# Delta-rule inverse: the transposed copy Y grown by a product per level, and the orders around it redone

## The reference, cut to what matters

```python
qkv, z, a, b = jnp.split(h @ w_in, [3 * W, 4 * W, 4 * W + H], axis=-1)
qkv = jax.nn.silu(causal_depthwise_conv(qkv, conv_w))
# per chunk of tokens, with decay = exp(gcum_i - gcum_j), kb = k * beta:
a_mat = jnp.where(strict, jnp.einsum('bhncd,bhnsd->bhncs', kb, kc) * decay, 0.0)
sol = lax.linalg.triangular_solve(a_mat, rhs, left_side=True, lower=True, unit_diagonal=True)
# ... scan over the chunks gives o; then
o = rms_norm_2(o, o_norm) * jax.nn.silu(z)
h = h + rms_norm_2(o @ w_out, post_norm)
```

## Time and profile before

| | us |
|---|---|
| median of 3 runs (lowest, highest) | 893.73 (893.17, 894.28) |
| the profiled execution's own time | 893.27 |
| its span, first to last instruction | 891.1 |
| PE busy, share of the span | 881.4, 99% |
| DVE busy | 632.1, 71% |
| ACT busy | 521.7, 59% |

### The profile page before, as it was taken

One profiled execution on the slowest core, in us unless ns is written; L12 is line 12 of the kernel. 1 busy time (PEld: TensorE's weight loads), 2 busy tenths in 40 slices (PEclk: granted clock), 3 DMA queues, 4 the chain that ended last, 5 costly groups with the idle time before them and its releaser, 6 DMA issues.

```text
span 891.1 us, 13047 instructions
## 1 busy us (share of the span) xinstructions
PE 881.4 (99%) x5231; PEld 767.6 (86%) x5231; DVE 632.1 (71%) x1067; ACT 521.7 (59%) x851; POOL 38.6 (4%) x48
## 2 busy tenths in 40 slices
PE   9999999999999999999999999999999999999997
PEld 8878888888888888888888888999989987798885
DVE  7986877766575667567656556679899867767774
ACT  6997443454445677645444435466556756747782
POOL 0151000000000000000000000000014310000000
PEclk9999999999999999999999999999999999999999
DMA  8722455454745454347455654555241312654511
GB/s 313 242 95 100 185 167 211 163 193 166 248 149 188 143 189 158 126 150 242 176 194 183 223 197 150 157 177 182 65 180 49 121 46 66 219 213 142 189 48 47
DMA packets 60876, 143.72 MB, mean 161 GB/s; under 512 B 4497, under 2 KB 6673, under 8 KB 60817
## 3 DMA queue, kind: packets, MB, share of 16 engines
q1 hardware_dynamic: 60816, 142.91, 46.3%
HBM read 141.85 MB, written 1.05 MB: 160 GB/s over the span
## 4 chain that ended last, share of the span: by engine, by line
PE 95%; DVE 2%; ACT 2%; DMA 1%; issue 0%; SPq 0%; DVEq 0%
PE ps L513 90%; PE ps L521 5%; ACT arena L1467 1%; DMA raw<-mla_w_in_dram 1%; ACT whi L1467 0%; DVE arena_r L2456 0%; DVE sub L2456 0%; DVE arena L2766 0%; DVE wlo L2456 0%; ACT xhl L1467 0%; DVE X L2462 0%; DVE st L2462 0%; ACT L1470 0%; DVE arena L2456 0%; DVE xhl L2462 0%
## 5 line engine op out<-in xcount | busy, mean ns | idle before, releaser
L2456 DVE TENSOR_TENSOR wlo<-raw,whi 128x2048 fp32r<-128x2048 f32 (+4 forms) x141 | 300.0, 2137 | 104.8 <-ACT whi L1467 104.7
L1467 ACT ACTIVATE whi<-raw 128x2048 fp32r<-128x2048 f32 (+6 forms) x143 | 251.6, 1771 | 158.5 <-PE ps L513 144.0
L513 PE MATMUL ps<-xhl,whi 128*128 128x512 f32 (+1 forms) x912 | 199.6, 346 | 0.0
L513 PEld LDWEIGHTS ps<-xhl,whi 128*128 128x128 f32 x912 | 155.1, 188 | 19.9 <-DVE xhl L2462 0.2
L513 PE MATMUL ps<-whi,xhl 128*128 128x512 f32 (+2 forms) x528 | 167.2, 385 | 0.4 <-DVE xhl L2462 0.3
L513 PE MATMUL ps<-whi,oth 128*128 128x512 f32 x416 | 165.4, 398 | 0.0
L513 PE MATMUL ps<-whi,otl 128*128 128x512 f32 x416 | 162.3, 390 | 0.0
L513 PE MATMUL ps<-wlo,oth 128*128 128x512 f32 x416 | 162.1, 390 | 0.0
L513 PE MATMUL ps<-xhl,wlo 128*128 128x256 f32 x704 | 121.6, 283 | 0.0
L513 PEld LDWEIGHTS ps<-whi,xhl 128*128 128x128 f32 x528 | 98.3, 189 | 18.4 <-issue 1.8
L513 PEld LDWEIGHTS ps<-xhl,wlo 128*128 128x128 f32 x704 | 103.0, 191 | 3.2 <-DVE wlo L2456 0.2
(11 more groups left out here) (150 smaller groups left out, 827.3 us busy)
## 6 DMA issues: line engine op xcount, KB each, us to landing
raw<-mlp_w_in_dram SPq DMA_DIRECT2D x32, 1024.0 KB, 5.3
raw<-mlp_w_out_dram SPq DMA_DIRECT2D x32, 1024.0 KB, 4.9
raw<-gdn_w_in_dram SPq DMA_DIRECT2D x16, 1024.0 KB, 5.3
raw<-moba_w_qkv_dram SPq DMA_DIRECT2D x12, 1024.0 KB, 5.1
raw<-kv_w_dram SPq DMA_DIRECT2D x8, 1024.0 KB, 5.4
raw<-fox_w_in_dram SPq DMA_DIRECT2D x8, 1024.0 KB, 5.1
raw<-mla_w_o_dram SPq DMA_DIRECT2D x4, 1024.0 KB, 4.8
raw<-moba_w_o_dram SPq DMA_DIRECT2D x4, 1024.0 KB, 6.2
```

The source lines that it names most:

```text
L513: return eng.matmul(o, l, r, start=start, stop=True, skip_group_check=True)
L1467: return eng.activation(o, i, f, **kw)
L2456: return eng.tensor_tensor(o, a, b, f)
```

## The change

`inv_v` becomes a product. As X grows by X*W, its transposed Y grows by the product of W and Y; PE forms that beside `inv_x`, from the same W, and DVE adds it to Y. ACT's `inv_y(g, l)` goes. Semaphore counts follow: DVE's `s_id[g]` now counts two steps a level, ACT's `s_ia[g]` one.

```diff
             def inv_x(g, l):
                 Xb, Yb, Wb, Bb = inv_ops(g)
-                L.wait_ge(s_ia[g], 2 * l - 4)
-                b = ring(("ix", g, l), s_id[g], l + 1)
+                L.wait_ge(s_ia[g], l - 1)
+                if l > 3:
+                    L.wait_ge(s_id[g], 2 * l - 3)
+                b = ring(("ix", g, l), s_id[g], 2 * l - 2)
...
             def inv_v(g, l):
-                Xf = inv_ops(g)[0].bitcast(F32)
-                L.wait_ge(s_id[g], l + 1)
-                b = ring(("iy", g, l), s_ia[g], 2 * l - 3)
+                Xb, Yb, Wb, Bb = inv_ops(g)
+                L.wait_ge(s_ia[g], l - 1)
+                b = ring(("iy", g, l), s_id[g], 2 * l - 1)
                 for s in blk4:
-                    ins = tr(P[b][:, s], Xf[:, s])
+                    ins = mm(P[b][:, s], Wb[:, s], Yb[:, s], True)
                 ins.then_inc(s_ip[g], 1)
...
-            def inv_y(g, l):
-                L.wait_ge(s_ip[g], 3 * l - 3 - g % 2)
-                act(inv_ops(g)[1], P[bank["iy", g, l]][:, :], ACT.Copy).then_inc(s_ia[g], 1)
...
+            def inv_v(g, l):
+                Yb = inv_ops(g)[1]
+                L.wait_ge(s_ip[g], 3 * l - 3 - g % 2)
+                tt(Yb, P[bank["iy", g, l]][:, :], Yb.bitcast(F32), ALU.add).then_inc(s_id[g], 1)
```

```diff
+            hi(108)
             decay(2)
-            hi(108)
             decay(3)
             decay(4)
             hi(109)
-            decay(5)
-            decay(6)
-            hi(110)
-            decay(7)
-            table("silu_and_others")
             conv_acc(10)
             conv_acc(11)
+            decay(5)
             v_silu(0)
+            table("silu_and_others")
+            decay(6)
+            decay(7)
             inv_0(1)
             inv_0(0)
             inv_w(0, 3)
+            hi(110)
             inv_w(1, 3)
-            inv_y(0, 3)
-            inv_y(1, 3)
             inv_w(0, 4)
+            z_silu(0, 0)
+            v_silu(1)
             inv_w(1, 4)
...
             table("natural_log_exp_and_others")
             rsq("gdn_o0")
+            sol(2, 3)
+            inv_w(3, 5)
+            inv_w(2, 5)
             sol(3, 3)
-            inv_y(3, 4)
-            inv_y(2, 4)
-            sol(2, 3)
-            inv_w(2, 5)
-            inv_w(3, 5)
+            out_squares(1)
+            z_silu(1, 1)
             out_hi(0)
-            out_squares(1)
-            inv_y(2, 5)
             inv_w(2, 6)
+            inv_w(3, 6)
             rsq("gdn_o1")
-            inv_y(3, 5)
-            inv_w(3, 6)
             inv_t(2)
...
             out_squares(2)
+            sol(7, 2)
+            sol(6, 3)
             rsq("gdn_o2")
-            sol(6, 3)
             sol(7, 3)
             out_squares(3)
             rsq("gdn_o3")
```

DVE's list: `conv_pre(11)`, `inv_0(2)` and `inv_b(0)` come earlier, `inv_e(3)` ahead of `inv_e(2)`, the additions of X and Y alternate, and near the end of groups 2 and 3:

```diff
+            inv_x(2, 6)
+            inv_v(3, 5)
             rsq_b("gdn_o1")
-            inv_x(2, 6)
+            inv_s(2)
+            inv_x(3, 6)
+            inv_f(2)
+            inv_s(3)
             out_norm(1)
```

More of the change, by code:

```diff
@@ L1251, in tensor_program @@
             to(106, 1)
+            kq(2)
+            to(106, 2)
             row_bc(3)
[L1253 to L1254 removed]
             row_bc(4)
+            to(107, 0)
+            kq(3)
             to(107, 1)
[L1257 removed]
+            row_bc(5)
             kq(4)
[L1259 removed]
             to(107, 3)
[L1261 removed]
             inv_c(0)
             row_bc(6)
+            kq(5)
             to(108, 0)
             inv_r(0)
+            to(108, 1)
             row_bc(7)
[L1267 removed]
             kq(6)
+            to(108, 3)
+            inv_0(0)
+            inv_0(1)
             to(109, 0)
[L1270 to L1271 removed]
+            inv_w(0, 3)
+            inv_w(1, 3)
             kq(7)
             to(109, 1)
[L1274 to L1275 removed]
+            inv_x(0, 3)
+            inv_v(0, 3)
             to(109, 2)
[L1277 removed]
             inv_x(1, 3)
[L1279 to L1286 removed]
+            v_T(0, 0)
+            inv_w(0, 4)
+            v_T(0, 1)
+            inv_v(1, 3)
+            inv_x(0, 4)
+            inv_v(0, 4)
+            inv_w(1, 4)
+            v_T(1, 0)
+            to(109, 3)
+            inv_w(0, 5)
             inv_x(1, 4)
[L1288 to L1289 removed]
             inv_v(1, 4)
+            to(110, 1)
             inv_w(1, 5)
[L1292 to L1294 removed]
+            inv_x(0, 5)
+            inv_v(0, 5)
             inv_x(1, 5)
[L1296 to L1297 removed]
+            to(110, 2)
+            inv_w(0, 6)
             inv_v(1, 5)
             inv_w(1, 6)
[L1300 to L1301 removed]
+            v_T(1, 1)
+            inv_x(0, 6)
             inv_x(1, 6)
[L1303 to L1305 removed]
             inv_f(0)
             inv_t(0)
+            inv_f(1)
             inv_c(1)
@@ L1323, in tensor_program @@
             inv_w(3, 3)
+            sol(1, 2)
             inv_w(2, 3)
             sol(3, 0)
-            sol(1, 2)
+            inv_x(3, 3)
             sol(0, 3)
-            inv_x(3, 3)
+            inv_v(3, 3)
+            inv_x(2, 3)
             sol(1, 3)
             sol(2, 1)
-            inv_x(2, 3)
-            inv_v(3, 3)
-            inv_w(3, 4)
             inv_v(2, 3)
             sol(3, 1)
+            inv_w(3, 4)
             inv_w(2, 4)
@@ L2291, in scalar_program @@
             inv_w(3, 3)
+            sol(1, 2)
+            sol(3, 0)
             inv_w(2, 3)
-            sol(3, 0)
-            sol(1, 2)
-            z_silu(1, 1)
             sol(0, 3)
@@ L3552, in vector_program @@
             block_(1)
+            decay_arg(2)
             conv_taps(9)
+            block_(2)
+            decay_arg(3)
+            lo(108)
+            decay_arg(4)
+            block_(3)
             inv_0(0)
[L3555 to L3558, removed]
+            decay_arg(5)
             conv_pre(10)
-            lo(108)
-            block_(3)
+            inv_0(1)
+            conv_pre(11)
             block_(4)
-            inv_0(1)
-            decay_arg(5)
             lo(109)
-            block_(5)
             inv_d(0)
             decay_arg(6)
+            block_(5)
+            inv_b(0)
             decay_arg(7)
-            inv_b(0)
-            conv_pre(11)
+            inv_e(0)
             inv_e(1)
+            inv_0(2)
             block_(6)
-            inv_e(0)
             conv_taps(10)
@@ L3577, in vector_program @@
             block_(7)
+            inv_x(0, 3)
             inv_0(3)
-            inv_x(0, 3)
+            inv_v(0, 3)
             inv_x(1, 3)
-            lo(110)
             v_beta(0, 0)
             v_beta(0, 1)
-            inv_0(2)
+            inv_v(1, 3)
+            inv_x(0, 4)
+            inv_v(0, 4)
+            lo(110)
+            v_beta(1, 0)
             inv_x(1, 4)
-            inv_x(0, 4)
-            v_beta(1, 0)
+            inv_v(1, 4)
             lo(111)
+            inv_x(0, 5)
+            inv_v(0, 5)
+            inv_x(1, 5)
+            lo(112)
+            inv_v(1, 5)
+            inv_x(0, 6)
             v_beta(1, 1)
-            inv_x(1, 5)
-            inv_x(0, 5)
-            lo(112)
             inv_x(1, 6)
+            inv_s(0)
             inv_s(1)
-            inv_x(0, 6)
-            inv_s(0)
+            inv_f(0)
             inv_f(1)
-            inv_f(0)
             inv_d(1)
@@ L3601, in vector_program @@
             inv_b(1)
+            inv_e(3)
+            sol(0)
             inv_e(2)
-            inv_e(3)
             inv_y(1)
             sol(1)
-            sol(0)
             lo(113)
             inv_x(3, 3)
+            inv_v(3, 3)
+            inv_x(2, 3)
             sol(2)
-            inv_x(2, 3)
+            inv_v(2, 3)
             sol(3)
@@ L3613, in vector_program @@
             inv_x(3, 4)
+            inv_v(3, 4)
             inv_x(2, 4)
             rsq_b("gdn_o0")
+            inv_v(2, 4)
             out_norm(0)
+            inv_x(3, 5)
             inv_x(2, 5)
+            inv_v(2, 5)
             out_lo(0)
-            inv_x(3, 5)
             out_sums(1)
+            inv_x(2, 6)
+            inv_v(3, 5)
             rsq_b("gdn_o1")
-            inv_x(2, 6)
+            inv_s(2)
+            inv_x(3, 6)
+            inv_f(2)
+            inv_s(3)
             out_norm(1)
[L3624 to L3627, removed]
             inv_f(3)
```

94 lines of the change are left out of this document (42 added, 52 removed).

## The result

The changed kernel takes 910.69 us (median of 4, 909.37 to 915.29) against 893.75 for the kernel before: a ratio of 1.0199, 95% interval 1.0162 to 1.0235. It is slower, as forecast, by 16.9 us where 12.3 were forecast; 910.69 lies at the upper end of the range. The profiled execution took 910.16, with a span of 908.0.

The account below looks back on a forecast made before the run. TensorE, busy 881.4 of 891.1 us, was taken as the bound. Products 0.1, first half 1.2, groups 2 and 3 1.9, later loads 3.1, 2.6, 2.2 and 1.2 sum to 12.3 over 893.27: 905.6 us, range 899.5 to 911.5.

Parts of the forecast that it names:

- 18 unnamed loads: ScalarE's new order breaks the table sets in two places, forcing 18 loads the program doesn't name, 1.28 us each.
- rival 1: One load per change of function family, so everything behind gdn_o1's load stays as before; 895.0 us, chance 0.09.
- Second place, behind the inversion: z_silu(1,1) behind the log-exp call: loads delay gdn_o2/gdn_o3 3.1, gdn_y0 2.6, gdn_y1 2.2, fox_x 0, forget_ln/fox_k0 1.2 us.
- Second place, in the inversion: Groups 2 and 3: a load for z_silu(1,1) and two for gdn_o1, about half in ScalarE's idle time; 1.9 us.
- First half: Groups 0 and 1: six additions on a nearly full VectorE, and v_T(1,0) waiting behind z_silu(0,0)'s load; 1.2 us.
- v_silu(0), decay(6), decay(7): Their loads fall into ScalarE's 27 idle us of 60; nothing, up to 1.3 us each without that cover.
- first place: v_silu(0) ahead of the silu call, decay(6) and decay(7) behind it; loads for v_silu(0), decay(6), z_silu(0,0).
- Copies and additions: ScalarE loses 12 copies, VectorE gains 12 additions; copies alone give nothing, a shorter chain returns at most 1.0 us.
- Second half (g 2 and 3): Loads for z_silu(1,1) and gdn_o1 in groups 2 and 3; 1.9 us, between -1.0 and 3.9.
- Rival 2: VectorE becomes the bound, six additions costing their whole 4.1 us, with the loads behind; 910.5 us, chance 0.08.
- Rivals 1 and 3: The third: not slower, shorter levels remove two TensorE waits and no load reaches TensorE; 892.3 us, chance 0.03.

Follow-up runs that it names:

- e1: Changed kernel with ScalarE's order mended in both places (decay(6), decay(7), silu call ahead of v_silu(0); z_silu(1,1) ahead of the log-exp call): 897.4 us.
- e13: e1 with one wait more: GpSimd's level(2,6) starts only when out_norm(0) is done, nothing left out: 895.1 us.
- e10: e1 with each of the 12 additions of Y done on 128 of its 512 columns: 897.93 us.
- e2: Changed kernel with z_silu(1,1) alone moved back ahead of the log-exp call: 900.14 us, 11 loads.
- e6: The change's products and additions in the orders of the kernel before, each addition behind its X addition or the next short step: 906.23 us.
- e3: Changed kernel with the log-exp table call written once more right behind z_silu(1,1): 901.99 us, 13 loads.
- e4: Kernel before, with z_silu(1,1) alone moved behind the log-exp call, no product or addition changed: 907.58 us.
- e5: Changed kernel with decay(6), decay(7) and the silu call ahead of v_silu(0); z_silu(1,1) stays behind the log-exp call: 911.1 us, 23 loads.
- e7: As e6, but with the redone orders, ScalarE's calls mended, for groups 0 and 1 alone: 902.39 us.
- e8: e1 with out_norm(0), out_T(0), out_hi(0) and out_lo(0) moved later in groups 2 and 3: 899.12 us.
- e11: e6 with each of the 12 additions of Y done on 128 of its 512 columns: 900.21 us.

## Why the prediction was wrong in size

- **18 unnamed loads of 1.28 us each, 26 in all: right,** and with them the direction. In the trace an unnamed load stands at each of the 18 places that were forecast. That agrees with the Trainium skill, by which a load comes ahead of every activation that needs one (ScalarE: Activation LUTs, "Table sets: the hidden batching unit"). The rule behind rival 1 (ScalarE activation tables: per-element evaluation and per-set limits, "Table sets in the compiler and the runtime") would, as the prediction read it, have made 13 loads; the trace doesn't agree with it here. From the start of a load to the start of what follows it on ScalarE it is 1.28 to 1.30 us at every load shown, so the price came from the row and not from the page.
- **Second place, behind the inversion: 9.1 forecast, 10.2 in the trace.** out_T(2) and out_T(3) 3.6 (3.1 forecast), turn_xf(0,0) 2.2 (2.6), turn_xf(1,0) 2.6 (2.2), fox_x 0.25 (0), c_T 1.5 (1.2). The slack of 0.36 that I subtracted at turn_xf(1,0) was there: the transposes start 2.35 later than the work ahead of them does. But behind the wait they take 0.61 to the next product's start (771.15 to 771.76) where they took 0.36 (756.24 to 756.60), and that makes the 2.6.
- **Second place, in the inversion: 1.9 forecast, 1.55 found** (6.62 - 5.07), and by the way that was forecast: VectorE waits for rsq("gdn_o1") with inv_s(2), inv_x(3,6) and inv_f(2) queued behind it, and TensorE for inv_x(3,6). VectorE's and TensorE's timelines in the kernel after:

```profile
725.10 0.17 DVE L2449 SCALAR_TENSOR_TENSOR st<-st 128x4 f32<-128x4 f32 x1 [1.69 <-ACT st L1470]
```

```profile
726.92 1.16 PE L513 MATMUL ps<-arena_r,arena 128*128 128x128 f32 x8 [1.35 <-DVE arena_r L2443]
```

- **First half: 1.2 forecast, 1.12 found** (e1 and e13), **but by luck.** The forecast took the 1.2 for the additions on a full VectorE and for v_T(1,0) behind the load of z_silu(0,0). e1 has no such load, and with additions of a quarter's length (e10) 0.91 of the 1.12 stays. TensorE's two waits there in e1 come to 0.78 (0.52 for a VectorE result, 0.26 for a ScalarE result). Whether the new order or the products in place of the transposes make the rest was not tested.
- **First failed step: "v_silu(0), decay(6), decay(7): ScalarE idles 27 of the 60 us; nothing."** The three loads of the first place cost 2.3 us in the trace. ScalarE's timeline shows how:

```profile
659.12 1.28 ACT L1470 ACT_TABLE_LOAD   x1
660.42 1.06 ACT L1470 ACTIVATE arena<-arena 128x1024 f32<-128x1024 f32 x1
661.50 1.28 ACT L1473 ACT_TABLE_LOAD   x1
662.78 1.28 ACT L1470 ACT_TABLE_LOAD   x1
664.08 0.47 ACT L1470 ACTIVATE arena<-ps,st 128x256 f32<-128x256 f32 x1
664.45 0.62 ACT L1470 ACTIVATE arena<-arena 128x512 f32<-128x512 f32 x1
```

TensorE's timeline at the two waits of the first place:

```profile
665.12 0.51 PE L513 MATMUL ps<-spread,pick 128*128 128x256 f32 x2 [1.04 <-ACT arena L1470]
...
682.79 0.66 PE L521 MATMUL ps<-small,arena 128*128 128x128 f32 x4 [1.39 <-ACT arena L1470]
```

  Three loads (two unnamed and the named one) and the Silu stand in one row between decay(5) and decay(6), 5.0 us, and row_bc(7) on TensorE starts 0.05 us behind the end of decay(6). ScalarE's 27 idle us lay elsewhere in the stretch. The wait at 682.79 is v_T(1,0) behind the load of z_silu(0,0), which the prediction named as a way but folded into the 1.2 of the first half.
- **Second failed step: in "Copies and additions" and "Second half (g 2 and 3)" the sum has no term for the additions and the new order in groups 2 and 3,** though half of the additions fall there; it put them at nothing without a reason. The arithmetic with its orders costs 1.65 us there at full clock (e2), of which about 1 is the collision of out_norm(0) with GpSimd (e13), and more in executions in which the clock falls. The 0.68 that stay without the collision were not taken apart.
- **The sum:** 2.3 for the first place's loads, 1.65 for groups 2 and 3, 1.1 behind the inversion, less 0.35 and 0.2 on the two terms of the inversion that came out lower (1.9 against 1.55; 1.3 with the products against 1.12): 4.5, the 16.8 of the trace less the 12.3 forecast.
- **The rivals.** Rival 2 (VectorE the bound) gave 910.5, nearly the time measured, and that is luck: its reason fell with e10, where additions of a quarter's length take as long as whole ones in e1. Rivals 1 and 3 fell with the 26 loads.

## What to carry to other kernels

Where a program names its activation tables by hand, each function must come while its set is the one last named: one Silu moved behind the call for Ln and Exp cost this kernel 14 us with no other change, and one more call behind it gave 8.7 back to the kernel after. An engine's idle share over a stretch is no cover for an instruction put into its queue; look at what the engine does just then and at who waits for the next thing in that queue. When steps are reordered on one engine, look also at what they will run beside on the others: a step that had fallen between two GpSimd products fell onto them.

## What the runs showed of the hardware that was not expected

- **VectorE and GpSimd block each other on some instructions.** An instruction of out_norm(0) takes some 0.35 us alone and up to 1.26 us while GpSimd multiplies a mask beside it, in after, e1, e2 and e6; four take 2.95 us in the kernel after, 1.13 in e13. The additions, whose one input is in PSUM, keep their 0.68 us beside the same GpSimd work. The Trainium skill (SBUF — State Buffer, "Who interferes with whom") says that a VectorE instruction with two inputs in SBUF contends with a GpSimd instruction that reads SBUF, and that the one issued first blocks the other. The traces agree: in the kernel after the first mask product starts 0.04 us behind an instruction of out_norm(0) and takes 1.32 us in place of 1.16, and the next two instructions of out_norm(0) take 1.26 and 1.25. GpSimd's timeline in the kernel after, and VectorE's:

```profile
715.91 2.49 POOL L3778 TENSOR_TENSOR arena_r<-arena,level_mask 128x512 fp32r<-128x512 f32 x2 [2.02 <-PE ps L513]
```

```profile
715.87 2.95 DVE L2449 SCALAR_TENSOR_TENSOR arena<-arena,st 128x128 f32<-128x128 f32 x4
```

- **TensorE's clock falls behind a stand in some executions and not in others.** In the profiled executions of e1, e3, e4, e5, e6, e7, e8 and e11 the granted clock goes to 0.50 (1.2 GHz of 2.4) for some 3 to 10 us behind a stretch around 716 to 722 in which TensorE was short of work. In e2's profiled execution (898.76 us) the same stand has no fall behind it, nor have the waits of about 1 us there in the kernel after and in e10:

```profile
718.00:720.00 2.00, 1.22 (x11) 1.06 (x10) 2.00 (x4) 0.32 (x1) 0.82 (x1) 1.00 0.82 308
720.00:722.00 2.00, 1.97 (x14) 1.56 (x12) 2.00 (x5) 1.23 (x2) 0.00 (x0) 1.00 0.04 13
```

  At the lower level a 128x512 product of chunk 111 starts every 0.43 us in place of 0.23. Groups 2 and 3 lose 4.18 us in e1's trace, with the fall (5.30 - 1.12), and 1.65 in e2's, without it, in the same order of work: the fall costs 2.5 us. Executions of one kernel spread by 3.3 us in e1 (895.93 to 899.23) and 5.9 in the kernel after (909.37 to 915.29), the slower ones mostly at a lower mean clock. What decides whether the clock falls was not settled.
